# Part of the second layer's conditioning on GpSimd beside the first FFN, with TensorE summing over rows

## What is computed

```python
def hybrid_layer(xl, xc, c, c_ctx, w_ada, b_ada, ..., with_ctx_out):
    mod_l = (jax.nn.silu(c) @ w_ada + b_ada)[:, None, :]      # w_ada: 1024 x 6144
    mod_c = jax.nn.silu(c_ctx) @ w_ada + b_ada
    sh1_l, sc1_l, g1_l, sh2_l, sc2_l, g2_l = jnp.split(mod_l, 6, -1)
    sh1_c, sc1_c, g1_c, sh2_c, sc2_c, g2_c = jnp.split(mod_c, 6, -1)
    hl = rms_norm(xl, norm_mix) * (1.0 + sc1_l) + sh1_l
    hc = rms_norm(xc, norm_mix) * (1.0 + sc1_c) + sh1_c
    ...                                                       # attention, mLSTM, pooling, w_out
    h2l = rms_norm(xl, norm_ffn) * (1.0 + sc2_l) + sh2_l
    xl = xl + g2_l * swiglu(h2l, w_ffn_gate, w_ffn_up, w_ffn_down)
    if with_ctx_out:                                          # layer 0 only
        ...                                                   # the same for xc
    return xl, xc
```

## Time and profile before

| what | value |
|---|---|
| median of 3 runs | 2044.31 us (2039.18 to 2044.73) |
| the profiled execution, its own time | 2039.42 us |
| its span, first to last instruction | 2037.4 us |
| PE busy | 1900.9 us (93%) |
| DVE busy | 1091.0 us (54%) |
| ACT busy | 759.4 us (37%) |
| POOL busy | 115.4 us (6%) |
| mean DMA | 131 GB/s |

### The profile page before, as it was taken

How to read it: one execution, slowest core, us unless ns; L and a number is a source line. 1 busy time by engine, 2 the same in 40 slices (tenths; PEclk the granted TensorE clock), 3 DMA queues, 4 the chain that set the end, 5 groups by cost and what they waited for, 6 DMA issues and landing times.

```text
span 2037.4 us, 34382 instructions
## 1 busy us (share of the span) xinstructions
PE 1900.9 (93%) x15088; PEld 1637.6 (80%) x15088; DVE 1091.0 (54%) x1685; ACT 759.4 (37%) x1060; POOL 115.4 (6%) x126
## 2 busy tenths in 40 slices
PE   6999888999999997988999999999998999899998
PEld 3767556777878777766899999989987777799997
DVE  3633565332333327556655576555666666566654
ACT  3432563222122224345433443343454433334332
POOL 1011001000000010000000100002001111000000
PEclk9999999999999999899999999999999999999999
DMA  8244211454354321203455555544431111145542
GB/s 334 91 163 160 74 52 63 165 184 157 104 181 171 114 84 52 94 1 106 152 180 178 178 211 184 169 165 145 156 141 37 43 43 43 64 166 186 186 168 81
DMA packets 37301, 266.22 MB, mean 131 GB/s; under 512 B 4128, under 2 KB 4256, under 8 KB 6816
## 3 DMA queue, kind: packets, MB, share of 16 engines
q1 hardware_dynamic: 36864, 260.87, 36.7%
q10 hardware_dynamic: 288, 3.15, 0.4%
HBM read 262.96 MB, written 1.05 MB: 130 GB/s over the span
## 4 chain that ended last, share of the span: by engine, by line
PE 85%; DVE 8%; ACT 4%; issue 1%; DMA 1%; SPq 0%; ACTq 0%; DVEq 0%
PE ps L585 20%; PE ps L586 20%; PE ps L587 20%; PE ps L2647 3%; PE ps L907 3%; PE ps L591 1%; PE ps L1468 1%; PE ps L1486 1%; PE ps L592 1%; PE ps L593 1%; DVE W L565 1%; PE ps L918 1%; PE ps L1255 1%; PE ps L1455 1%; PE ps L2193 1%
## 5 line engine op out<-in xcount | busy, mean ns | idle before, releaser
L565 DVE TENSOR_TENSOR W<-ring,W 128x2048 fp32r<-128x2048 f32 (+2 forms) x194 | 430.9, 2223 | 290.4 <-ACT W L556 290.1
L556 ACT ACTIVATE W<-ring 128x2048 fp32r<-128x2048 f32 (+2 forms) x194 | 359.3, 1854 | 136.9 <-PE ps L587 129.9
L585 PE MATMUL ps<-h_lat,W 128*128 128x256 f32 x1056 | 301.7, 286 | 4.1 <-DVE h_lat L732 4.0
L586 PE MATMUL ps<-h_lat,W 128*128 128x256 f32 x1056 | 299.8, 284 | 0.0
L587 PE MATMUL ps<-h_lat,W 128*128 128x256 f32 x1056 | 299.7, 284 | 0.0
L585 PEld LDWEIGHTS ps<-h_lat,W 128*128 128x128 f32 x1056 | 203.5, 193 | 5.5 <-issue 4.6
L586 PEld LDWEIGHTS ps<-h_lat,W 128*128 128x128 f32 x1056 | 203.8, 193 | 0.3 <-issue 0.2
L587 PEld LDWEIGHTS ps<-h_lat,W 128*128 128x128 f32 x1056 | 203.7, 193 | 0.0
L890 DVE TENSOR_TENSOR work<-work,ps 128x256 f32<-128x256 f32 (+1 forms) x88 | 43.0, 488 | 211.8 <-ACT work L865 211.7
L585 PE MATMUL ps<-hidden_lat,W 128*128 128x256 f32 x528 | 150.4, 285 | 6.3 <-DVE hidden_lat L893 6.3
L587 PE MATMUL ps<-hidden_lat,W 128*128 128x256 f32 x528 | 150.1, 284 | 0.0
(11 more groups left out here) (363 smaller groups left out, 4004.9 us busy)
## 6 DMA issues: line engine op xcount, KB each, us to landing
ring<-w_up_dram SPq DMA_DIRECT2D x88, 1024.0 KB, 4.9
ring<-w_ada_dram SPq DMA_DIRECT2D x48, 1024.0 KB, 4.9
ring<-w_down_dram SPq DMA_DIRECT2D x43, 1024.0 KB, 4.9
ring<-w_rkv_dram SPq DMA_DIRECT2D x13, 1024.0 KB, 4.8
ring<-w_fm_dram SPq DMA_DIRECT2D x10, 1024.0 KB, 5.0
ring<-w_out_dram SPq DMA_DIRECT2D x8, 1024.0 KB, 4.9
ring<-w_gates_dram SPq DMA_DIRECT2D x8, 1024.0 KB, 4.8
ring<-w_qk_dram SPq DMA_DIRECT2D x6, 1024.0 KB, 5.0
```

What stands on the lines that cost most here:

```text
L556: act.activation(slots[SLOT[s]][:, 0, 0:cols], ring[:, u % RING, 0:cols], ACT.Copy).then_inc(w_high, 1)
L565: dve.tensor_tensor(slots[SLOT[s]][:, 1, 0:cols], ring[:, u % RING, 0:cols], slots[SLOT[s]][:, 0, 0:cols], ALU.subtract).then_inc(w_low, 1)
L585: pe.matmul(o, slots[SLOT[s]][:, 0, at:at + cols], high, start=first, stop=False)
L586: pe.matmul(o, slots[SLOT[s]][:, 0, at:at + cols], low, start=False, stop=False)
```

## The change

Of layer 1's 24 conditioning units, TensorE keeps the first 8 (those needed for both token kinds). The other 16 are computed by GpSimd, for the latent column only: it loads half units of 128 x 1024 itself, from its own queue, into two new buffers (`p_ring`), multiplies by the conditioning column (spread over 256 columns), and halves the result by additions until 128 x 256 are left in `p_sum`. It starts when all pieces of the norm ahead of the FFN are written (`h_low`). TensorE then sums a unit over the 128 rows by two matmuls with a column of ones, behind up tiles 1 to 16, one unit behind each; it waits for GpSimd's count `p_acc` there. `p_sum` has two buffers: GpSimd starts unit x (x at least 2) after TensorE took unit x-2 (`p_taken`). The 8 units kept are spread anew: they follow tiles 2, 4, 7, 9, 12, 14, 17 and 19. The ring's list loses 16 loads.

```diff
-    PHASES += [(f"ada{_l}", "raw", [UNIT] * ADA_UNITS), ...
+    PHASES += [(f"ada{_l}", "raw", [UNIT] * (ADA_UNITS if _l == 0 else ADA_FIRST)), ...
...
 def ada_at_tile(t):
-    return range(min(ADA_UNITS, t * ADA_UNITS // ADA_TILES_1), min(ADA_UNITS, (t + 1) * ADA_UNITS // ADA_TILES_1))
+    return range(min(ADA_FIRST, t * ADA_FIRST // ADA_TILES_1), min(ADA_FIRST, (t + 1) * ADA_FIRST // ADA_TILES_1))
...
                     if r == 0:
-                        for a in ada_at_tile(hidden_done(0, x, i)):
+                        tile = hidden_done(0, x, i)
+                        if 1 <= tile <= ADA_UNITS - ADA_FIRST:
+                            pe.wait_ge(ada_rows, ADA_UNITS + max(ada_at_tile(tile - 1).stop, 0))
+                            pe_ada_sums(pe, tile - 1)
+                        for a in ada_at_tile(tile):
                             pe_ada_unit(pe, ADA_UNITS + a)
                 if r == 0 and x == len(FFN_PARTS[0]) - 1:
-                    pe_ada_fold(pe, 2 * ADA_UNITS - 1)
+                    pe_ada_fold(pe, ADA_UNITS + ADA_FIRST - 1)
...
+        p_ring = a(2 * UNIT // 2).rearrange("p (b n) -> p b n", b=2)
+        p_sum = a(2 * ADA_COLS).rearrange("p (b n) -> p b n", b=2)
...
+        def pool_load(pool, n):
+            pool.dma_start(p_ring[:, n % 2, :], dram["w_ada1"][ADA_FIRST + n // 2, :, n % 2 * UNIT // 2:(n % 2 + 1) * UNIT // 2])\
+                .then_inc(p_in[n % 2], 16)
...
+        def pool_ada(pool):
+            units = ADA_UNITS - ADA_FIRST
+            pool_load(pool, 0)
+            pool_load(pool, 1)
+            pool.wait_ge(h_low, H_DONE[1] + PIECES[1])
+            for n in range(2 * units):
+                x = n // 2
+                pool.wait_ge(p_in[n % 2], 16 * (x + 1))
+                if n % 2 == 0 and x >= 2:
+                    pool.wait_ge(p_taken, x - 1)
+                w = p_ring[:, n % 2, :]
+                c = cond[:, n % 2 * HALF:(n % 2 + 1) * HALF, 1:2].broadcast_to([P, HALF, ADA_COLS])
+                half = w.rearrange("p (k c) -> p k c", k=HALF)
+                plink(pool.tensor_tensor(half, half, c, ALU.mult))
+                plink(pool.tensor_tensor(w[:, 0:2 * ADA_COLS], w[:, 0:2 * ADA_COLS], w[:, 2 * ADA_COLS:], ALU.add))
+                if n % 2:
+                    plink(pool.tensor_tensor(w[:, 0:ADA_COLS], w[:, 0:ADA_COLS], p_sum[:, x % 2, :], ALU.add))
+                pool.tensor_tensor(p_sum[:, x % 2, :], w[:, 0:ADA_COLS], w[:, ADA_COLS:2 * ADA_COLS], ALU.add).then_inc(p_acc, 1)
+                pool.wait_ge(p_acc, n + 1)
+                if n + 2 < 2 * units:
+                    pool_load(pool, n + 2)
+
+        def pe_ada_sums(pe, x):
+            pe.wait_ge(p_acc, 2 * x + 2)
+            for m in range(2):
+                at = ADA_FOLD + 4 * (ADA_FIRST + x) + 2 * m + 1
+                mm = pe.matmul(ps[:, 7, at:at + 1], p_sum[:, x % 2, m * P:(m + 1) * P], K("ones")[:, 0:1], start=True, stop=True)
+            mm.then_inc(p_taken, 1)
...
                 pool_sums(pool, 2 * layer + 1)
+                if layer == 0:
+                    pool_ada(pool)
                 pool_sums(pool, 2 * layer + 2)
```

More of the change, by code:

```diff
@@ L175 @@
 for _l in range(DEPTH):
-    PHASES += [(f"ada{_l}", "raw", [UNIT] * ADA_UNITS), (f"tma{_l}", "split", [KT // 2 * TMA] * 2),
+    PHASES += [(f"ada{_l}", "raw", [UNIT] * (ADA_UNITS if _l == 0 else ADA_FIRST)), (f"tma{_l}", "split", [KT // 2 * TMA] * 2),
                (f"fm{_l}", "split", [UNIT] * 4 + [UNIT // 2, UNIT]), (f"tmb{_l}", "split", [KT // 2 * TMB] * 2),
@@ L957, in pe_ada_fold @@
             mm = ada_fold(pe, x, x % ADA_UNITS)
-            if (x + 1) % ADA_UNITS == 0:
+            if x in (ADA_UNITS - 1, ADA_UNITS + ADA_FIRST - 1):
                 mm.then_inc(ada_cols, 1)
@@ L965, in pe_ada_unit, with plink @@
             ada_products(pe, x, 7)
+        a = Area(HIDDEN + max(FFN_PARTS[0]) * 2 * TA, FIXED)
+        p_ring = a(2 * UNIT // 2).rearrange("p (b n) -> p b n", b=2)
+        p_sum = a(2 * ADA_COLS).rearrange("p (b n) -> p b n", b=2)
+        p_in = [sem(f"p_in{b}") for b in range(2)]
+        p_acc, p_taken = sem("p_acc"), sem("p_taken")
+        HALF = KT // 2
+        def pool_load(pool, n):
+            pool.dma_start(p_ring[:, n % 2, :], dram["w_ada1"][ADA_FIRST + n // 2, :, n % 2 * UNIT // 2:(n % 2 + 1) * UNIT // 2])\
+                .then_inc(p_in[n % 2], 16)
+        def plink(ins):
+            links["pool"](ins)
+        def pool_ada(pool):
[25 more added lines that the diff above has]
+            mm.then_inc(p_taken, 1)
         def act_copy(act):
```

## The result

The changed kernel is faster: 2030.06 us median of nine runs (2021.91 to 2033.64) against 2042.16 for the kernel before (2039.07 to 2049.82), ratio 0.9929 with a 95% interval of 0.9915 to 0.9944. By that ratio it is 14.5 us (11.4 to 17.4 by the interval). The prediction had given 2046.3 and called no change the likeliest; the time lies at the lower edge of its range, 2030 to 2063, and on the side to which it gave 0.26.

A forecast was written before the change was run, and what follows sets the result against it. TensorE was taken to set the first FFN's pace; 10 U - 145.6 + max(0, 4 U - 59.7) gave +0.4 us, with the clock's 1.6 +2.0, so 2041.4 for the profiled execution and 2046.3 median, range 2030 to 2063.

The forecast's parts named there:

- no change: Whole kernel: no measurable change, the forecast itself, with 14.1 to 14.9 us per GpSimd unit; chance 0.38.
- TensorE's gain if GpSimd is never late: First FFN's up tiles: down starts 8.3 us earlier and the second part saves 8.6, together 17 us.
- The tensor operations: GpSimd's two multiplications, five additions and seven hand-overs per unit: 9.6 us, or 10.4 with the dearer multiplication.
- The issues: GpSimd issuing two transfers per unit itself: 0.8 us each, 1.6 a unit (0.7 to 2.6).
- The exclusion: DVE's split, low part and cast in each up tile block GpSimd, which loses nearly all of 3.4 us.
- The sum: GpSimd's unit time set against TensorE's pace over both parts: +0.4 us, +2.0 with the slower clock.
- U: Time GpSimd takes for one conditioning unit: 14.6 us, also break-even; the full gain needs below 12.9.
- The slope of 10: First part: each us of GpSimd's unit time moves the kernel's time by 10 us.
- The formula's constant: Start of the first down projection: late by 10 U - 137.0 us, where 137.0 is the constant.
- The range: Whole kernel, 8 in 10: 2030 to 2063 us, from U = 13.1 (about -14) to U = 15.9 (+19).
- The clock: Start of the down projection: after PE idles, the clock falls to 1.2 GHz instead of 2.4, losing 1.6 us.
- The fast one: GpSimd keeps up better, by cheap issues or DVE meeting gaps: U = 12.8 gives the full 17 us; chance 0.26.

The follow-up runs named there:

- the shorter multiplications: The changed kernel with each GpSimd multiplication cut into two over 512 columns; median 2042.76 us, ratio 1.0000.
- the hold: The changed kernel, but GpSimd starts unit 10 only when the eleventh hidden tile is written; medians 2034.08 us (ratio 0.9958), repeat 2032.20 (0.9936).
- the hold and later sums: The changed kernel with GpSimd's unit 10 held for the eleventh hidden tile and each sum one tile later; medians 2025.39 us (0.9917), repeat 2026.72 (0.9907).

## Why the prediction was wrong

- **TensorE's gain if GpSimd is never late, 17 us.** Right, 1.5 too small: 18.5 with GpSimd's work left out. A sum alone costs 391.48 - 380.09 - 10.95 = 0.44 (I took 0.5). Up tiles 11 to 21 took 128.87 against a predicted 129.4.
- **The tensor operations, 9.6.** Slightly dear: 1.92 for the multiplication (2.0), 0.08 per hand-over (0.12), so 9.0. By the slope of the additions the multiplication would have taken 2.4.
- **The issues, 1.6.** A little cheap: 0.59 each, and 0.30 ahead of each in which GpSimd's queue waits for its own last addition; with a hand-over of 0.02 that is 1.8 a unit. The landing, 4.1, was right, and it stayed hidden.
- **The exclusion, 3.4. This is the step that failed**: "since GpSimd is never idle in this stage it loses nearly all of that once per tile". The exclusion itself is there, for the cast too (0.43 alone, up to 2.55 beside a multiplication), and it works both ways. But it costs GpSimd 1.6 a unit. Of each DVE operation about 0.36 is not lost, part of it the hand-over of 0.08 that GpSimd spends anyway, and of the split 0.83 more, which falls on an issue and its wait (0.91). The same split cost GpSimd 1.08 with an issue beside it, 1.92 with a hand-over only, and 2.14 when it began just ahead of an addition. Even with no issue beside it the three together can cost only about 3.41 - 3 x 0.36 = 2.3, which the shorter multiplications reached, and not 3.4. The Trainium skill, "SBUF — State Buffer", section Who interferes with whom, says that an operation of DVE with two inputs takes the shared pair's read side only and that making a transfer's descriptors needs the write side, which it calls inferred; the trace agrees (0.59 with the split running). I had cited that section for the lock and for transfers that suffer, and not read it for transfers that go on.
- **The sum.** U was 12.43 instead of 14.6, and this 2.2 times ten, 1.8 of it from the exclusion, turned a gain into a forecast of none. The slope of 10 held (9.7). The formula's constant was about 6 us too low, for the first unit and the seam; with that put right it gives part 1 as 147.6 + 124.3 - 137.0 + 6 = 140.9, and 141.1 was measured. It also moves the point from which the gain shrinks from U = 12.9 to 12.3: the changed kernel sits just at it, its tenth sum 1.6 late. The two errors worked against each other, and had U been 14.6 as predicted the kernel would have been slower by about 8, not by 2: its stage lies 1.9 above the one before with U = 14.02 and 16.4 above it with 15.25.
- **The range.** Its fast side, U = 13.1, was given as about -14, but the prediction's own sum with the clock's 1.6 gives -13.0, that is 2031.3, and 2030.06 lies outside that. That the time falls inside the stated range is luck.
- **The clock.** A halved stretch at the start of down came as forecast, though the wait was for DVE and not for GpSimd, and it cost 2.7, not 1.6. Ahead of it PE idled 3.56 us behind a sum, against 1.26 before, when no such stretch followed. What decides it is not shown: the idle of 2.3 us ahead of the second down projection was followed by a stretch at the lower level before, and by none after.
- **Rivals.** The fast one happened, for its second reason (DVE goes in the gaps) and not its first (issues near 0.33).

## What to carry to other kernels

When two engines exclude each other, the price is not the length of the other's operations but what of them falls on operations of one's own: lay them side by side in time, and look for issues and hand-overs that they can use. A helper engine near the pace of the main one has a knee, here at about 12.3 us a unit; find the knee first and then ask how sure the pace is, for on this kernel half a microsecond more of arithmetic per unit made the unit 1.2 longer and took 10 us of the stage away. Read a local change by the span of its stage: that repeats within 0.1 us, while the same code ahead of it took from 346.9 to 356.7 us in the profiled executions in which the norm is undisturbed, and the code behind it 1277.7 to 1284.5.

## What the runs showed of the hardware that was not expected

- GpSimd's issue of a 512 KB transfer to 128 partitions took 0.54 to 0.72 us in 32 instances (median 0.59), and the transfer landed in 4.1, the same as one of SP's. The twelve issues that ran beside DVE's split, an operation with two inputs, took 0.59 too.
- An operation of DVE and one of GpSimd that exclude each other overlap a little at each change: a DVE operation that waited cost GpSimd 0.36 less than its own length, hand-over included (the split of 2.29 cost 1.92).
- A multiplication on GpSimd over 512 columns took 1.10, an addition over 512 took 1.29; a multiplication over 1024 took 1.92.
- The total of stretches at the lower clock differs between executions and kernels in code that is the same: what lies behind the stage took 1277.7 and 1277.8 in two executions of the changed kernel, 1283.1 and 1282.9 in two with the hold, and 1280.4 and 1277.8 in two with the hold and later sums. It stays open why.
